# Two transformer blocks on one Trainium2 core: the second block's mixer with its weight units interleaved among the state space scan and the attention

## The reference, cut to what matters

```python
u = _rmsnorm(h, mix_pre_g)
proj = u @ w_in                                   # 2048 x 7728 columns
(u_ssm, q, kc, vc, ksl, vsl, kw, vw, g_nsa, g_a, g_b) = jnp.split(proj, split_at, axis=-1)
y_ssm = jax.nn.gelu(_s5(u_ssm, ...))              # state space scan: 64 groups x 64 complex states
y_a = (y_ssm @ ssm_glu_w1) * jax.nn.sigmoid(y_ssm @ ssm_glu_w2)
o_nsa = _nsa(q, kc, vc, ksl, vsl, kw, vw, g_nsa, ...)   # compressed, selected and window attention
y_b = o_nsa @ nsa_w_o
mixed = (jax.nn.sigmoid(g_a) * y_a + jax.nn.sigmoid(g_b) * y_b) @ w_out
h = h + _rmsnorm(mixed, mix_post_g)
```

## Time and profile before

| | |
|---|---|
| median of 3 runs | 3950.0 us (3949.53 to 3953.66) |
| the profiled execution | 3949.08 us, its span 3947.0 us |
| TensorE matmul busy | 3554.3 us, 90% of the span |
| VectorE busy | 2142.4 us, 54% |
| ScalarE busy | 1468.0 us, 37% |
| GpSimd busy | 213.4 us, 5% |
| mean granted TensorE clock | 0.928 |
| moved by DMA | 699.36 MB, 177 GB/s |

### The profile page before, as it was taken

One profiled execution on the slowest core, in us unless ns is written; L12 is line 12 of the kernel. 1 busy time (PEld: TensorE's weight loads), 2 busy tenths in 40 slices (PEclk: granted clock), 3 DMA queues, 4 the chain that ended last, 5 costly groups with the idle time before them and its releaser, 6 DMA issues.

```text
span 3947.0 us, 57793 instructions
## 1 busy us (share of the span) xinstructions
PE 3554.3 (90%) x23666; PEld 3285.3 (83%) x23666; DVE 2142.4 (54%) x2332; ACT 1468.0 (37%) x1507; POOL 213.4 (5%) x351
## 2 busy tenths in 40 slices
PE   1997889999999799999997889667999989999998
PEld 1884679988998699889987877446999789989996
DVE  7876568754655544444445233696544454444444
ACT  0332345543443333333334224233343343333333
POOL 1110000000000000000000000353000000000000
PEclk8898889999999899999998885578999989999999
DMA  9995559756665566566654740002666556656663
GB/s 395 312 370 165 194 178 273 220 186 191 181 181 189 147 181 181 191 192 181 181 192 129 162 121 2 1 1 69 181 180 188 181 149 181 181 192 191 181 182 138
DMA packets 830981, 699.36 MB, mean 177 GB/s; under 512 B 12519, under 2 KB 762399, under 8 KB 823216
## 3 DMA queue, kind: packets, MB, share of 16 engines
q1 hardware_dynamic: 811984, 627.09, 53.6%
q0 software_dynamic: 18736, 71.08, 5.5%
q10 hardware_dynamic: 176, 0.07, 0.0%
HBM read 692.93 MB, written 5.26 MB: 177 GB/s over the span
## 4 chain that ended last, share of the span: by engine, by line
PE 84%; DVE 8%; DMA 2%; ACT 2%; issue 2%; POOL 1%; DVEq 0%; SPq 0%; ACTq 0%; POOLq 0%
PE ps L1782 17%; PE ps L1783 17%; PE ps L1784 17%; PE ps L1807 8%; PE ps L1808 8%; PE ps L1811 8%; DMA stage<-in_w_ada 1%; PE ps L2171 1%; PE ps L2094 1%; DVE w_lo L1042 1%; ACT w_hi L699 1%; PE ps L2155 1%; PE ps L2115 1%; DMA stage<-in_w_in 1%; DVE acc L1181 1%
## 5 line engine op out<-in xcount | busy, mean ns | idle before, releaser
L1042 DVE TENSOR_TENSOR w_lo<-stage,w_hi 128x2048 fp32r<-128x2048 f32 (+1 forms) x536 | 1211.1, 2260 | 1415.0 <-ACT w_hi L699 1414.8
L699 ACT ACTIVATE w_hi<-stage 128x2048 fp32r<-128x2048 f32 (+1 forms) x536 | 1012.2, 1889 | 1767.2 <-PE ps L1784 1122.4
L1782 PE MATMUL ps<-xt_hi,w_hi 128*128 128x256 f32 x5440 | 1552.6, 285 | 34.1 <-DVE w_lo L1042 25.4
L1783 PE MATMUL ps<-xt_lo,w_hi 128*128 128x256 f32 x5440 | 1548.9, 285 | 0.0
L1784 PE MATMUL ps<-xt_hi,w_lo 128*128 128x256 f32 x5440 | 1548.4, 285 | 0.0
L1782 PEld LDWEIGHTS ps<-xt_hi,w_hi 128*128 128x128 f32 x5440 | 1054.6, 194 | 38.1 <-DVE w_lo L1042 23.8
L1783 PEld LDWEIGHTS ps<-xt_lo,w_hi 128*128 128x128 f32 x5440 | 1054.6, 194 | 0.1
L1784 PEld LDWEIGHTS ps<-xt_hi,w_lo 128*128 128x128 f32 x5440 | 1054.1, 194 | 0.0
L1807 PE MATMUL ps<-w_hi,hid_hi 128*128 128x512 f32 x1184 | 462.1, 390 | 7.4 <-DVE w_lo L1042 7.4
L1808 PE MATMUL ps<-w_lo,hid_hi 128*128 128x512 f32 x1184 | 461.6, 390 | 0.0
L1811 PE MATMUL ps<-w_hi,hid_lo 128*128 128x512 f32 x1184 | 365.2, 390 | 0.0
(11 more groups left out here) (356 smaller groups left out, 3091.4 us busy)
## 6 DMA issues: line engine op xcount, KB each, us to landing
stage<-in_w_in SPq DMA_DIRECT2D x92, 1024.0 KB, 5.7
stage<-in_w_up SPq DMA_DIRECT2D x88, 1024.0 KB, 5.7
stage<-in_ffn_w_gate SPq DMA_DIRECT2D x88, 1024.0 KB, 5.6
stage<-in_ffn_w_up SPq DMA_DIRECT2D x88, 1024.0 KB, 5.6
stage<-in_ffn_w_down SPq DMA_DIRECT2D x88, 1024.0 KB, 4.9
stage<-in_w_ada SPq DMA_DIRECT2D x48, 1024.0 KB, 7.4
stage<-in_w_down SPq DMA_DIRECT2D x44, 1024.0 KB, 4.9
late<-in_w_ada POOLq DMA_DIRECT2D x64, 512.0 KB, 6.9
```

Source lines behind the costliest of these rows:

```text
L699: act.activation(w_hi[:, u % 2 * UNIT:u % 2 * UNIT + n], stage[:, u % SLOTS * UNIT:u % SLOTS * UNIT + n], ACT.Copy).then_inc(hi_made, 1)
L1042: dve.tensor_tensor(w_lo[:, part], stage[:, u % SLOTS * UNIT:u % SLOTS * UNIT + n], w_hi[:, part].bitcast(F32), ALU.subtract).then_inc(spl ...
L1782: pe.matmul(dst, wh, chunk(xh, k0 + k), start=start and k == 0, stop=False)
L1783: pe.matmul(dst, wh, chunk(xl, k0 + k), start=False, stop=False)
```

## The change

**The order.** The projection's 28 units and the 32 units of gates a and b (`gg`) make one unrolled stretch of 60 units t. The scan is cut into 16 slots of three units (`slot_start`, one extra unit at slot 8), begun at t = 7; its steps are written between the units on each queue. Then come 16 units of glu weights (each now 8 chunks x 2 columns of tiles, `pair_tile`), written between compression, compressed attention and the attention loop (half a unit in every second round), and 8 units of `nsa_w_o` (`wo`) after it.

**Buffers.** The scan's tables move out of the weights' buffers into `pt2`'s surroundings, the norm's `f_nat`, `row` and `turn`. For that `trig`, `z`, `backs`, `cw` and the drive's PSUM banks have one buffer in place of two. `x_nat` is written to DRAM (2 MB) before the mixer and read back after it; the 32 gate tiles go to DRAM through `sg_out` (128 KB each, from ScalarE's queue) and are read back in two loads of 2 MB to `sg_a` and `sg_b`; the compressed bias goes out and back too.

**Work that changes.** GpSimd subtracts and adds its products (two more operations for a pair), so `read` has 4 matmuls for 8 and `make_c` 8 small writes for 12. The second glu factor's sigmoid is made from ScalarE's exponential (`glu_exp`), an addition and a reciprocal of 512 columns on VectorE (`glu_rest`). The bias tables and the 3 MB write move to the second block's first feed-forward (`up10`). The queries' scaling goes into the tile copy; `out2` waits for `mixed_made` unit by unit.

```diff
+def slot_start(s):
+    return 7 + 3 * s + s // 8
...
+        for t in range(60):                              # TensorE
+            pe.wait_ge(S["tile_copied"], 20 + t - 2)
+            if t < 28:
+                tile_unit("in2", 0, 0, t, bank(TILE_BANK[t % 3], 0, T), norm_index=None if t else 3)
+            else:
+                tile_unit("gg", 0, 0, t - 28, bank(TILE_BANK[t % 3], 0, T))
...
+            for s in range(17):
+                at = slot_start(s)
+                if t == at and s:
+                    read(s - 1)
+                elif t == at + 1 and s < 15:
+                    drive(s + 1)
+                elif t == at + 2 and s < 14:
+                    bring(s + 2)
...
+            for s in range(16):                          # VectorE, after split(t)
+                at = slot_start(s)
+                if t == at + 1:
+                    turn_in(s)
+                elif t == at + 2:
+                    scans(s)
+                elif t == at + 3:
+                    if s % 2 == 0 and s >= 2:
+                        sum_y(s // 2 - 1)
+                    if s < 14:
+                        angle(s + 2)
+                    if s % 2 == 0:
+                        make_c(s // 2)
+                    elif s >= 3:
+                        rest_y((s - 3) // 2)
...
+        for pr in range(16):                             # GpSimd
+            pool.wait_ge(S["scan_made"], pr + 1)
+            if pr:
+                pool.wait_ge(S["y_made"], pr)
+            for k, (w, z) in enumerate(((cosine, z_r), (sine, z_i), (cosine, z_i), (sine, z_r))):
+                last = pool.tensor_tensor(part[k], w[:, at], z[:, :], ALU.mult)
+            last.then_inc(S["back_made"], 1)
+            pool.wait_ge(S["back_made"], pr + 1)
+            pool.tensor_tensor(part[0], part[0], part[1], ALU.subtract)
+            pool.tensor_tensor(part[2], part[2], part[3], ALU.add).then_inc(S["xs_made"], 1)
+            if pr % 2 and pr <= 11:
+                pool.wait_ge(S["xs_made"], pr + 1)
+                spread_b((pr + 3) // 2)
...
+        pool.wait_ge(split_used, plan["gg"][1] + 34)
+        for s in range(4):
+            pool.wait_ge(sg_sent[s], 16 * 8)
+        for v, to in enumerate((sg_a, sg_b)):
+            pool.dma_start(to[:, :].rearrange("p (k n) -> p k n", n=T),
+                           sg_dram[v * KC:(v + 1) * KC].rearrange("k p n -> p k n")).then_inc(S["sg_in"], 16)
...
+        compress(0)                                      # TensorE, after the 60 units
+        glu(0)
+        glu(1)
+        compress(1)
+        turn_hidden(0)
+        glu(2)
+        turn_hidden(1)
+        glu(3)
...
+            if i % 2 == 0 and 4 <= i < 28:               # TensorE, attention round i, after the scores
+                glu_tile(7 + i // 4, i // 2 % 2)
...
+        def glu_rest(p):                                 # VectorE
+            dve.wait_ge(S["glu_e"], p + 1)
+            link.then(dve.tensor_scalar(x, x, 1.0, None, ALU.add))
+            link.then(dve.reciprocal(x, x))
+            dve.tensor_tensor(part, part, x, ALU.mult).then_inc(S["glu_r"], 1)
```

More of the change, by code:

```diff
@@ L379, in fetch_merge @@
-        def fetch_merge(i, u):
-            to = slot(u).rearrange("p (k n) -> p k n", n=P)
-            if u < 2:
-                return [(to, in2[:, :, ds(i * P + (GA_IN2, GB_IN2)[u], P)])]
-            at = i * P if isinstance(i, int) else (i + 1) * P - P
-            if u == 2:
-                return [(to[:, 8 * v:8 * v + 8], halves[v][:, :, ds(at, P)]) for v in range(2)]
-            return [(to[:, 0:8], halves[2][:, :, ds(at, P)])]
-        load("merge", 4, 16, fetch_merge)
+        load("gg", 4, 8, tiles(I["w_in_2"], GA_IN2))
@@ L1011, in _ @@
+        for w in range(2, 8):
+            split("wo", 0, 0, w)
+            mixed_hi(w - 2)
         for u in range(16):
             split("out2", 16, 0, u)
+            if u < 2:
+                mixed_hi(6 + u)
             if u == 12:
@@ L1749, in take_out2 @@
+        for w in range(2, 8):
+            split("wo", 0, 0, w)
+            if w > 2:
+                mixed_lo(w - 3)
+            mixed_sum(w - 2)
         def take_out2(half):
@@ L2031, in _, with glu, turn_hidden @@
+        def glu(g):
+            for tile in range(2):
+                glu_tile(g, tile)
+        def turn_hidden(x):
             pe.wait_ge(S["hn_gelu"], x + 1)
@@ L2159, in read @@
-        def read(pr):
-            c = pr // 2
-            if pr % 2 == 0:
-                pe.wait_ge(S["cw_made"], c + 1)
-                if c:
-                    pe.wait_ge(S["y_sum"], c)
-            pe.wait_ge(S["back_made"], pr + 1)
-            for e in range(2):
-                jj = 2 * (pr % 2) + e
-                for x, wsel in enumerate((0, 1, 2, 2)):
-                    a = (c % 2) * 1536 + wsel * 512 + jj * P
-                    last = pe.matmul(bank(7, 0, T), cw[:, a:a + P],
-                                     backs[pr % 2][:, x * 512 + e * T:x * 512 + (e + 1) * T],
-                                     start=pr % 2 + e + x == 0, stop=pr % 2 + e == 2 and x == 3)
-            last.then_inc(S["y_made"], 1)
@@ L2215, in _ @@
-        merge(0, True)
-        with pe.Fori(1, 16) as i:
-            merge(i, False)
-        pe.wait_ge(S["mixed_made"], 16)
-        rows_phase("out2", 8, hid_hi, hid_lo)
+        glu(15)
+        pe.wait_ge(S["on_lo"], 4)
+        pe.wait_ge(S["av_taken"], 8)
+        for w in range(8):
+            if w == 2:
+                pe.wait_ge(S["glu_a"], 8)
+            elif w == 3:
+                pe.wait_ge(S["glu_e"], 8)
+            elif w >= 4:
+                pe.wait_ge(S["wo_sum"], w - 3)
+            for tile in range(2):
+                pair_tile(plan["wo"][1] + w, tile, bank(4 + w % 4, tile * T, T), po_hi, po_lo, w % 2)
```

1179 lines of the change are left out of this document (636 added, 543 removed).

## The result

| | before | after |
|---|---|---|
| median of the runs, us | 3951.8 (4 runs, 3949.5 to 3956.8) | 3757.0 (4 runs, 3755.4 to 3760.3) |
| ratio, with its 95% interval | | 0.9506 (0.949 to 0.9523) |
| profiled execution: span, us | 3947.0 | 3754.7 |
| first matmul of the second tile, us | 2118.41 | 2153.18 |
| first matmul of `out2`, us | 3063.26 | 2869.37 |

The kernel is 195 us faster. From `out2` to the end the two executions take the same (883.7 and 885.3 us), so the whole difference lies ahead of it.

The account below looks back on a forecast made before the run. TensorE, 90% busy, was taken as the bound, so only time without weight work could be won. Stage terms put `out2` at 2940 in place of 3063, 123 us less: 3826 us, own range 3775 to 3885, 8-in-10 range 3762 to 3925.

Parts of the forecast that it names:

- 24.0 us a slot: Scan slots of three units: mean of even and odd pairs 23.2 plus 0.8; 16 slots and an extra unit, 384 + 5.8.
- The hand-over: Scan slots: 0.8 us added to each slot for handing over between queues.
- The odd slot: Scan slot after an odd pair: VectorE 21.0 us, TensorE's 22.0 the longer and so taken.
- The blocking: Scan slots: GpSimd's products delay VectorE, next split 3.6 us (waits 1.3, runs 2.3), five angle instructions about 6.2.
- TensorE's pace: Rival: scan slots run at TensorE's 22.0 us and the clock stays up, attention 121; total 3760, chance 0.17.
- the third rival: Clock falls to 0.50 in the scan slots, 38.2 us a slot; total 4050, slower than before; chance 0.08.
- The rival of 29 us a slot: VectorE and GpSimd never overlap in the scan slots, 29 us each with hand-overs; total 3906, chance 0.2.
- I take 155, the middle: Attention loop: 155 us, between 183 at a clock of 0.50 and 121 at 1.00.
- the warm case: Attention loop at clock 1.00: some 111 us, plus 10 for `glu_rest` and splits that hold VectorE, 121.
- waits 26: Compression and compressed attention: 26 us of waits on top of 46 for glu units and 38 of other TensorE work.
- The stall on the gates: Compressed stage: gate tiles back from DRAM about 40 us after tile 59, stalling 11 us.
- Start: Second projection tile to unit 7: 34.6 us of units, 5.8 of gate columns, some 7 of small work.

Follow-up runs that it names:

- angle_act: The changed kernel with the first two steps of the scan's angles moved from VectorE to ScalarE; 0.9481 of before.
- read_one: The changed kernel with one matmul a pair in the scan's `read` in place of four; 3748.1 us.
- attention_alone: The changed kernel with glu units 8 to 13 taken out of the attention loop and run dense behind it; 3777.2 us, 0.9544 of before.
- rev_small: The changed kernel with the reversed bias rows written 16 times, not 128, and the strips read in eight transfers; 0.9464 of before.

## Why the prediction was right in direction and wrong in size

Three terms of the sum were mis-sized and make nearly all of the difference: the slot of the scan, the attention loop and the waits of the compressed stage.

**The scan slots, -35.** "24.0 us a slot" was a walk of 24.4 after an even pair and 22.0 after an odd one, and 0.8 for handing over. In after, slots alternate between 23.3 and 21.0, and their mean, with some shorter ones, is 22.0: 16 x 2.0 = 32 us. Three parts of the step failed:

- The hand-over, 0.8 a slot, is not there beside the 0.27 us that the split waits after an even pair: VectorE's instructions follow each other while TensorE works ahead out of two buffers.
- The odd slot was raised from VectorE's 21.0 to TensorE's supposed 22.0, by taking the larger of two engines in each slot, 0.5 in the mean. With two weight buffers an engine that is ahead in one slot carries it into the next, and TensorE's own need is 21.2 (`angle_act`). The carrying is read from the slots' times, 23.3 and 21.0, neither of them raised to the other engine's need; no run changes the buffers.
- After an even pair VectorE's small work (`sum_y` and `make_c`) takes 2.8 us and not 3.4, turning and recurrences 6.1 and not 6.6, and this makes the 23.3.

The blocking itself was nearly right where it was charged: angles 6.2, measured 6.5 and 6.9; the split after an even pair 3.6, measured 0.27 and 3.3. That the odd slot of VectorE came out at its 21.0 is luck. Its split was priced at 3.6 and takes 2.3, since it is ahead of the product; and the walk had left out `rest_y` (1.4 us under GpSimd's products) and 0.7 of the angles.

The rival with slots at "TensorE's pace" had the number, 22.0, but mostly the wrong engine, as `read_one` shows. Its total of 3760 is 3 us from the measured 3757, and this is luck too: its attention was 14 us too short and its compressed stage 16 too long. The forecast's range began 2 us above this rival's own total. Two more of the prediction's figures are slips: its own range would begin at 3780, not 3775, and the third rival comes to 4053, not 4050. The rival of 29 us a slot fell. It needed GpSimd's time never to overlap VectorE's; but GpSimd is idle 41% of the slots, the splits and turnings beside its small copies (`bn`) keep their 2.28 and 0.68 us, and its products meet no turning in after. In `angle_act` 14 turnings that read PSUM do meet products and keep their 0.68 us.

**The attention, -20.** "I take 155, the middle" between 183 cold and 121 warm: the term that was mis-sized, with 135.0 measured. `attention_alone` shows that the mechanism was right: without dense units 1.2 GHz throughout, with them mostly 2.4 GHz. The loop has warm rounds as in the warm case. It is 14 us over 121 by a first wait of 6.7 us, by the cold rounds up to 2690.6, and by three stops of 3.1, 3.1 and 4.1 us with a cold round behind each; for `glu_rest` and the splits the warm case had 10 us in its 121. The first wait is the one that the forecast had put at 7 us into the compressed stage (VectorE's last `glu_rest` and split ahead of the first maximum). By the forecast's own border the loop took 128 and was 27 us too long in the forecast, and the compressed stage 10.

**The compressed stage, -16.** Of "waits 26" the trace shows 6.2 in the stage, and the 7 just named behind it; TensorE's work took 87.4 us where 84 were forecast. All of TensorE's waits in the stage (total us, times, longest):

```profile
PE ps L2267 <- DMA stage<-in_cmp_v_w: 3.5, 1, 3.5
PE ps L1939 <- DVE w_lo L1131: 1.8, 1, 1.8
PE ps L2374 <- DVE o_nat L1831: 0.9, 1, 0.9
```

The stall on the gates, 11 us, did not come: their load was issued 4.2 us behind tile 59 and landed 24.5 behind it, not 40, and TensorE had work until then. The 1.8 us ahead of the third glu unit are a wait for its weights, which ScalarE got only at 2604.20. `rev_small` brought a stall on the gates, 6.3 us, by another cause than the forecast's: not the transfer's length, the time at which it starts. So this term was a real risk that the order of after just avoids.

**Start -6, feed-forward +7.** The small VectorE work between the first units costs 1.4 us and not 7 (41.8 less six units and the gates, 40.4): TensorE was busy 41.8 of 41.8. In the feed-forward the two holes cost 12.4 and 17.1 us, 29.5 against 28. The first is the idle time of 15.92 us at 1450.83 less the usual 3.54; the second is what the three splits from 1502.67 to 1537.07 take over three units of 5.76. Of the rest, 4.0 us were there at 969.9 already (965.9 before), ahead of anything the change touches, and executions differ there by as much. Parking x cost nothing that shows.

**Tail, +1.5**, and clock in the slots 1.00: right. Of the signs named beforehand these did not come: the stall ahead of the third glu unit was 1.8 us and not 5 to 15, and not released by the gates' load; VectorE was at 96% in the slots and not 80, TensorE at 98 and not 90; and `w_lo` splits were longer behind six of the 16 recurrences only.

The differences add because nearly all had one sign: each uncertain wait was charged, and where two clocks were possible their mean was taken.

## What to carry to other kernels

When two engines share a pipeline with two buffers, compare their sums over many slots, not the larger of the two in each slot, and do not add a hand-over. Where matmuls of small tiles run at 1.2 GHz with TensorE already busy, dense work interleaved with them is worth more than the idle time that it fills: six units cost 14 us in the loop and 35 behind it. A 2 MB load on GpSimd's queue, harmless in one place, leaves TensorE waiting for weights twice for over 11 us in another; place it by the traffic and not only by the date on which it is needed.

## What the runs showed of the hardware

The blocking between VectorE and GpSimd goes both ways and is decided by who starts first: 0.16 us of lead turned a split of 3.31 into one of 2.28, and a product of 1.3 into 3.27. TensorE, 98% busy in the loop of `attention_alone`, was granted 1.2 GHz for 108 us on end, and the clock had fallen to it while TensorE was busy without a gap. And eight transfers of 256 KB, begun just behind 4 MB of gates, took 27.8 us each to land (12.4 when issued 43 us behind the gates' loads), while the second compression's weights of 1 MB on SyncE's queue took 16.2 us (12.0 in after, where only the gates are beside them; the first compression's took 5.3; each the median of two).
